# Two engines share the multiplication by the post norm's root, in a three-block network on one core

## The reference, cut to what matters

```python
def rms_norm(x, g):
    x32 = x.astype(jnp.float32)
    y = x32 * lax.rsqrt(jnp.mean(x32 * x32, axis=-1, keepdims=True) + EPS)
    return (y * g.astype(jnp.float32)).astype(x.dtype)
...
        x = x + rms_norm(m, g[1])
        f = conv_glu_ffn(rms_norm(x, g[2]), ffn_w_in[i], ffn_conv_w[i], ffn_conv_b[i], ffn_w_out[i])
        x = x + rms_norm(f, g[3])
        gate = jax.nn.sigmoid(rms_norm(x, g[4]) @ ple_w_gate[i])
        x = x + gate * (p[i] @ ple_w_proj[i])
```

## Time and profile before

| | us |
|---|---|
| median of three runs | 2586.79 |
| lowest and highest | 2583.77, 2590.02 |
| the profiled execution, its time | 2586.66 |
| the profiled execution, its span | 2584.9 |
| TensorE matmul busy | 2473.4 (96%) |
| VectorE busy | 1522.6 (59%) |
| ScalarE busy | 1008.4 (39%) |
| GpSimd busy | 154.7 (6%) |
| mean granted TensorE clock, of full speed | 0.987 |

### The profile page before, as it was taken

The page is one execution under the profiler, slowest core; times in us unless marked ns, Lnnn a source line. Parts: engine busy times, 40 slices in busy tenths (PEclk is TensorE's granted clock), DMA queues, the critical chain, the costliest instruction groups (busy, mean ns, idle before and its releaser), DMA issues.

```text
span 2584.9 us, 29179 instructions
## 1 busy us (share of the span) xinstructions
PE 2473.4 (96%) x11538; PEld 1974.3 (76%) x11538; DVE 1522.6 (59%) x2379; ACT 1008.4 (39%) x1547; POOL 154.7 (6%) x166
## 2 busy tenths in 40 slices
PE   6999998999997999998999999999999999999998
PEld 4878886877865888886777688887777767888876
DVE  5976435677667333346655755544857668555346
ACT  4223233444545332233444433333546554333333
POOL 0000111000010000010001000010100010000100
PEclk9999999999999999999999999999999999999999
DMA  9556427532212333232321223232232112322321
GB/s 371 172 179 204 152 90 148 109 62 51 69 54 73 98 98 98 90 106 70 102 74 65 82 98 98 94 109 84 81 103 87 64 49 82 98 98 94 100 92 65
DMA packets 233705, 265.90 MB, mean 103 GB/s; under 512 B 8377, under 2 KB 222009, under 8 KB 233569
## 3 DMA queue, kind: packets, MB, share of 16 engines
q1 hardware_dynamic: 220704, 223.39, 28.5%
q0 software_dynamic: 11088, 37.46, 4.3%
q10 hardware_dynamic: 1776, 3.18, 0.3%
HBM read 259.78 MB, written 10.75 MB: 105 GB/s over the span
## 4 chain that ended last, share of the span: by engine, by line
PE 65%; DVE 6%; issue 3%; ACT 3%; POOL 0%; DMA 0%; POOLq 0%; ACTq 0%; DVEq 0%
PE G L2051 56%; PE X L2051 1%; DVE wl L1346 1%; PE G L2506 1%; PE X L2486 1%; ACT yh L820 1%; DVE yl L1372 1%; DVE h L1435 1%; PE G L2444 1%; PE X L2411 1%; PE X L2495 1%; DVE tmpA L1387 1%; PE X L2247 0%; PE X L2425 0%; ACT wh L771 0%
## 5 line engine op out<-in xcount | busy, mean ns | idle before, releaser
L1346 DVE TENSOR_TENSOR wl<-raw,wh 128x1024 fp32r<-128x1024 f32 (+1 forms) x398 | 474.6, 1199 | 673.0 <-ACT wh L771 672.6
L2051 PE MATMUL G<-yh,wh 128*128 128x512 f32 x1864 | 754.1, 405 | 43.0 <-DVE yl L1364 15.7
L2051 PE MATMUL G<-yh,wl 128*128 128x512 f32 x1864 | 732.1, 393 | 0.0
L2051 PE MATMUL G<-yl,wh 128*128 128x512 f32 x1864 | 731.3, 392 | 0.0
L771 ACT ACTIVATE wh<-raw 128x1024 fp32r<-128x1024 f32 (+1 forms) x398 | 410.0, 1037 | 808.1 <-PE G L2051 788.3
L2051 PEld LDWEIGHTS G<-yh,wh 128*128 128x128 f32 x1864 | 353.5, 190 | 142.9 <-issue 27.4
L2051 PEld LDWEIGHTS G<-yl,wh 128*128 128x128 f32 x1864 | 353.2, 189 | 76.5
L2051 PEld LDWEIGHTS G<-yh,wl 128*128 128x128 f32 x1864 | 353.8, 190 | 71.4 <-issue 2.4
L2051 PE MATMUL G<-hidh,wh 128*128 128x512 f32 x704 | 275.6, 391 | 0.0
L2051 PE MATMUL G<-hidl,wh 128*128 128x512 f32 x704 | 273.9, 389 | 0.0
L2051 PE MATMUL G<-hidh,wl 128*128 128x512 f32 x704 | 273.9, 389 | 0.0
(11 more groups left out here) (351 smaller groups left out, 2993.2 us busy)
## 6 DMA issues: line engine op xcount, KB each, us to landing
raw<-in_ffn_w_in SPq DMA_DIRECT2D x44, 1024.0 KB, 4.9
raw<-in_ffn_w_gate SPq DMA_DIRECT2D x22, 1024.0 KB, 5.3
raw<-in_ffn_w_up SPq DMA_DIRECT2D x22, 1024.0 KB, 5.2
ada_c<-in_ada_w POOLq DMA_DIRECT2D x20, 1024.0 KB, 5.4
raw<-in_ffn_w_down SPq DMA_DIRECT2D x16, 1024.0 KB, 5.3
raw<-in_w_in SPq DMA_DIRECT2D x16, 1024.0 KB, 9.4
raw<-in_ffn_w_out SPq DMA_DIRECT2D x16, 1024.0 KB, 5.2
ada_z<-in_ada_w SPq DMA_DIRECT2D x14, 1024.0 KB, 10.9
```

Of the source, the lines that this page charges most:

```text
L1346: nc.vector.tensor_tensor(place(wl), src, f32(place(wh)), ALU.subtract).then_inc(lo, 1)
L2051: ins = nc.tensor.matmul(bank, a, b, start=first and i == 0, stop=last and i == 2)
```

## The change

In the five `post` stretches GpSimd multiplies tiles 2 to 7 of the branch by `R`, behind its `add_squares`. It waits until the root is there, until ScalarE has squared all of `yo` (`yy_ready`) and until VectorE has read its last tile (`hy_last`), and counts `yr_ready` once per tile. VectorE multiplies tiles 0 and 1, and waits for `yr_ready` ahead of the adds of tiles 2 to 7. TensorE's, ScalarE's and SP's lists are what they were.

```diff
@@ GpSimd's program
+            def times_root(e):
+
+                yo = yo_att if e in (7, 12) else yo_ffn
+                pool.wait_ge(rstd_ready, e + 1)
+                pool.wait_ge(yy_ready, KT * (POST[e] + 1))
+                pool.wait_ge(hy_last, POST[e] + 1)
+                for k in range(2, KT):
+                    nc.gpsimd.tensor_tensor(yo[:, k, :], yo[:, k, :], R[:, :], ALU.mult).then_inc(yr_ready, 1)
+
...
                 if norm == "post":
                     add_squares(e, KT - 1)
+                    if e + 1 not in FULL:
+                        times_root(e)
@@ VectorE's program, in post()
                 def times_root(k):
-                    st.step(nc.vector.tensor_tensor(yo[:, k, :], yo[:, k, :], R[:, :], ALU.mult))
+                    if k < 2:
+                        st.step(nc.vector.tensor_tensor(yo[:, k, :], yo[:, k, :], R[:, :], ALU.mult))
 
                 def add_h(k):
                     st.wait()
+                    if k >= 2:
+                        dve.wait_ge(yr_ready, (KT - 2) * (POST[e] - len(FULL)) + k - 1)
                     nc.vector.tensor_tensor(h[:, k, :], h[:, k, :], yo[:, k, :], ALU.add).then_inc(h_ready, 1)
```

More of the change, by code:

```diff
@@ L221, in build @@
         acc_init = sem("acc_init")
+        yr_ready = sem("yr_ready")
         most_mm = sem("most_mm")
```

## The result

The change makes the kernel slower by 1%: 2612.8 us (median of six, 2611.3 to 2614.2) against 2589.3 for the kernel before on the same chip (median of six, 2583.8 to 2594.7), ratio 1.0097 with a 95% interval of [1.0086, 1.0108]. The forecast was 2608.9 us, slower, in a range of 2597 to 2618. The profiled execution took 2612.4 us, 25.7 more than that of the kernel before; the prediction's sum was +22.2.

What follows compares the result with a forecast made beforehand. TensorE, 96% busy, was taken to lose time waiting on the VectorE-ScalarE chain in the five posts. Blocks of VectorE add 2 x 5.2 + 4.5 + 2 x 3.65 = 22.2 us to 2586.66: 2608.9, range 2597 to 2618.

Steps and rivals of the forecast that it cites:

- What bounds the kernel, and that the removed work is worth 0: Posts: add, upper part, lower part chain delays TensorE; 20.7 us of multiplications leaving VectorE lie in waits, worth 0.
- A block of 1.03 to 1.07 for each of GpSimd's instructions: Five posts: each GpSimd multiplication keeps VectorE out 1.03 to 1.07 us; 1.08 taken.
- Posts 7 and 12, 5.2 each: Add 2 comes 10.91 us behind the root instead of 5.74; 5.2 us slower per post.
- Post 5, 4.5: Other storing order, lower part spacing 1.06; add 2 at 12.0 us instead of 7.5, 4.5 slower.
- The walks: Step-by-step counts per post of VectorE and GpSimd alternating from the root; 5.2, 4.5 or 3.65 us slower each.
- Posts 9 and 14, 3.65 each: VectorE also writes weights' lower part; TensorE's tile 1 starts at 11.5 us instead of 7.87, 3.65 slower.
- The fourth rival: TensorE's clock falls behind new waits in posts 9 and 14, 1.5 us per spell: +3, 2612; chance 0.12.
- The first case: The forecast itself: blocks make the five posts slower, +22 us, 2608.9; chance 0.55.
- The second rival: GpSimd needs over 0.61 us between multiplications, so VectorE gets two instructions in: 12 us, 2598.7; chance 0.15.
- The third: Each block lasts GpSimd's whole record of 1.35 us: 8.1 more, 2617; chance 0.10.
- The fifth: No slower: VectorE goes first or blocks end within its 0.79 wait, 2586.7; chance 0.06.
- Costed at nothing: New waits for yr_ready, and GpSimd's first attention DMAs moving from 1166.0 to about 1179.5: 0 us.

Runs made afterwards that it cites:

- e1: Kernel before with the multiplication of tiles 2 to 7 left out on both engines and a maximum in the mean square's last step: 2585.8 us, ratio 0.9999.
- e6: Kernel before, GpSimd not multiplying, with VectorE's add of tile k+1 moved ahead of the lower part of tile k: 2575.9 us, ratio 0.9959.
- e3: VectorE multiplies all eight tiles as in the kernel before; GpSimd only writes zeros into twelve unused tiles per post: 2584.7 us, ratio 0.9998.
- e4: The change with GpSimd multiplying only tiles 5, 6 and 7, VectorE tiles 0 to 4: 2598.0 us, ratio 1.005.
- e10: VectorE multiplies all as in the kernel before; GpSimd runs six unread multiplications per post of two different tiles: 2612.5 us, ratio 1.0112.
- e2: VectorE multiplies all as in the kernel before; GpSimd multiplies R by R into unused tiles six times per post: 2604.4 us, ratio 1.0083.
- e9: The change, but in posts 9 and 14 GpSimd's first multiplication also waits for the weights' lower part behind tile 0: 2599.1 us, ratio 1.0061.
- e5: The change, but GpSimd's multiplication of tile k waits for VectorE's add of tile k-2: 2592.4 us, ratio 1.0035.
- e7: The change together with e6's order of VectorE's adds: 2595.1 us, ratio 1.0038 against the kernel before.
- e11: VectorE multiplies all as in the kernel before; GpSimd runs six single-input copies of the root per post: 2595.8 us, ratio 1.0044.
- e12: e6 with VectorE's multiplication moved one tile further ahead, GpSimd not multiplying: 2577.2 us, ratio 0.9967 against the kernel before.

## Why the prediction came out as it did

- **What bounds the kernel, and that the removed work is worth 0**: right. e1 shows it by itself (0.9999), and e6 from the other side: the chain was one of order between VectorE and ScalarE, and taking a link out of it gave 10 us, while taking VectorE's work away gave nothing.
- **A block of 1.03 to 1.07 for each of GpSimd's instructions, taken from two adds**: right, with 1.08 taken. Post 7 has starts 1.68 apart for a hold of 0.61 to 0.67, so 1.07 behind a multiplication or an add and 1.00 behind a lower part; e3 shows that reading is what blocks, e4 that the cost goes with the number.
- **Posts 7 and 12, 5.2 each**: 5.06. **Post 5, 4.5**: 4.08. The walks held; the old pace of 2.15 came back as forecast.
- **Posts 9 and 14, 3.65 each**: 6.15 and 6.14. This is the term that was mis-sized. VectorE's walk held: it had the weights' lower part done 8.0 us behind the root, and TensorE started on it at 8.07 (1821.93 against a root that ended at 1813.86); it had lower part 1 at 11.44, and it ended at 11.39. From 8.07 TensorE has fifteen matmuls to run before tile 1, 3.4 us at 0.227 each, which would have been 11.5, as forecast. They took 5.93. The 2.5 us between are the lower clock. With that left out the five posts would come to 2 x 5.06 + 4.08 + 2 x 3.65 = 21.5, the forecast's 22.2 within 1.
- **The fourth rival, the clock**, was therefore not a rival but a part of the outcome: it had the place and the mechanism right, was given 0.12, and priced at 1.5 per spell from a window of 3 us at 0.50. Here the spell went on at 0.65 for 3 us more, 1.5 + 1.05 us. With it the sum is 22.2 + 5 = 27.2, where the posts show 26.5. So what came is the fourth case and not the first, at more than its price, with the sign that the prediction had named for it, a clock of 0.5 in posts 9 and 14. The first case's 2608.9 came near the measured 2612.8 with both spells missing from it; the fourth's 2612 is nearer. e10 and e2 show that the step isn't certain from the waits alone: same waits, one post with it and one without.
- **The second rival** (GpSimd over 0.61 between two): fell; six in 10.18 with 1.07 each leave 0.63 per gap, and in that gap VectorE got one instruction in, not two. That gap is VectorE's own hold. What GpSimd itself needs is less: in e9 the fourth of the six starts while VectorE waits for ScalarE, at 1822.09, and the next at 1823.34, 1.25 behind it, which leaves 0.18 behind a block of 1.07. **The third** (the block lasts the whole record): fell. The Trainium skill, SBUF — State Buffer, section SBUF: two separate sides, has the engine that starts first keep the shared pair "for the whole instruction"; the rows show a little less than that, 1.00 to 1.07 of the 1.29 to 1.35 that GpSimd's instruction reads when it runs alone (1.30 in e5). **The fifth** (no slower): fell in every post.
- **Costed at nothing**: none of VectorE's waits was ended by the counts of yr_ready, and GpSimd's DMAs went out at 1176.6, far ahead of their reader.

What stays open: why 3 us of the profiled difference lie at a lower clock near 1320 to 1350. The kernel before, e1, e2 and e3 have 1.00 there, the changed kernel and the other nine 0.89 (e7 0.94); since e6 and e12 are among these and e2 is not, it isn't GpSimd's multiplications that bring it. What decides whether TensorE's clock falls behind two waits is open too. And only GpSimd's side was varied: whether a VectorE instruction with one input in SBUF would be kept out wasn't tried.

## What to carry to other kernels

Work that lies in an engine's wait is worth nothing when it leaves, and before moving it, look whether the new engine takes something from the old one: here each of GpSimd's two-input instructions kept VectorE out for 1.00 to 1.07 us, more than the 0.61 that a multiplication takes of VectorE's time. If such work must be on GpSimd, start it behind whatever the next engine is waiting for: the same six multiplications cost 6.15 us at the head of post 9 and 0 behind its first tile, where TensorE had work of its own to bound the stretch. And when the chain alternates between two engines, first try the order on the engine that has work left to put in between; that was worth 10 us here.

## What the runs showed that was not expected

- How long GpSimd keeps VectorE out depends on what it reads: 1.00 to 1.07 us for two different tiles of 128 x 512, 0.72 to 0.84 for one tile named twice (e2), 0.35 to 0.41 for a copy (e11), nothing for writing (e3).
- Two engines that each need what the other holds alternate one for one: in e10 GpSimd's six took 10.17 us, in the change 10.18, though VectorE had other instructions beside them.
- The same two waits, 1.93 and 1.26 us, were followed once by a granted clock of 1.00 and once by 0.50 in one execution (e10); the lower clock cost 1.95 us in that post. In e2 the waits of 1.16 and 1.02 were followed once by 0.57 over 3 us and once by 1.00, 1.20 us apart.
- A post on VectorE can end sooner while the kernel gains nothing: in e12 posts 7 and 12 are 0.75 us shorter than in e6, but TensorE starts later, and the time from their roots to the next ones is the same.
